# Normalising x by token, evacuating the projection on ScalarE, and turning plain x inside the mix product

## The chip, the core and the metric

One NeuronCore of a Trainium2 chip runs the whole program. Its engines are TensorE (PE, with its weight loads PEld), VectorE (DVE), ScalarE (ACT), GpSimd (POOL) and SyncE (SP, which only issues DMAs here; ACT issues some too). The metric is the device time of one execution in microseconds, as a median over runs: 3062.14 us for the kernel before (three runs, 3060.99 to 3066.02).

## What is computed

One encoder block, float32, on 2048 tokens of width 1024, with 256 memory tokens:

```python
h = rmsnorm(x, mix_norm_w);  proj = h @ w_in          # 1024 -> 3072: q k v g a b, 512 each
y_ret  = retention_group(q, k, v, g, ...)             # 4 heads of 128, both directions, chunks of 128
y_conv = conformer_conv_group(a, b, ...)              # a*sigmoid(b), 31-tap depthwise conv, layernorm, silu
x = x + concat([y_ret, y_conv]) @ w_out               # "mix"
x = x + cross_attention(rmsnorm(x), rmsnorm(mem))     # 4 heads of 256, 256 memory tokens
x = x + square(relu(rmsnorm(x) @ w_ff1)) @ w_ff2      # 1024 -> 4096 -> 1024
return rmsnorm(x, final_norm_w)
```

Each big product keeps float32 accuracy by splitting both sides in a high and a low part: hi*hi, hi*lo and lo*hi, so 24 matmuls of 128x128 by 512 columns for one 128x512 output ("a GEMM" below).

## The kernel before

Activations lie with features on partitions and tokens along the free axis: 8 tiles of features (k), 4 chunks of 512 tokens (n). Five instruction streams are written by hand; every order is explicit and is kept by semaphores. Weights come as 128x1024 blocks through two slots `wraw`; POOL splits each block (`split_weights`, L505: `whi` L511, `wlo` L513), and a slot's turn comes when the block before it in that slot has been used.

**Prologue** (L283 to L350, L673 to L696, L1013 to L1035, L1366 to L1386). x is loaded in token-major halves of chunks (`xt`), turned by PE (L679), and each turned tile in PSUM is read four times: ACT makes `xhi` (times the norm weight, L1022) and squares it (`sq0`, L1024), DVE copies plain x to `xf` (L1371, which SP stores to `xT_d`, L350) and makes `xlo` (L1372); POOL adds the squares (L543). The same is done for mem. PE sums the squares over features (L692), ACT and DVE turn that into 1/rms as a full tile `rs` (L1033, L1383). The first projection GEMM comes after all of it (L696). x in these products is not normalised.

**Projection** (L701 to L768, a loop over 4 heads c). `ORDER` (L55) lists the items of a head: six groups of four GEMMs (a, b, q, k, v, g), memory products V and K (256 columns), O (values through `w_xo`) T and M (`w_xq` turned and multiplied by the keys). PSUM banks 0 to 3 are used in turn, one semaphore `bank_free` in order; banks 4 to 7 hold O and M. DVE evacuates every GEMM with `ps * rs` (`evac`, L1393), into `upad` for a, into `st` for the others; ACT then stores `st` to `proj_d` (L1042), or takes the sigmoid of b (L1087), and DVE multiplies a by it (L1464). Between these DVE runs the 31 taps of the convolution (`tap`, L1419), two after each evacuation. DVE also makes the low parts of K and V (`low`, L1403), of w_xq (`query_low`, L1407) and of the stored products (`made_low`, L1415). `values_out` (L713) waits for `w_ready`, that is the low part too; `keys_in` (L740) waits for `query_low`.

**Retention and convolution** (L772 to L866). The loads of k, its swapped halves, v, q, q swapped and g for head 0 are issued by SP from L393 on, after the last store of the memory products (L390). sin and cos are loaded earlier (L386).

**Two halves of 1024 tokens** (L876 to L990): mix (`product`/`mix`, L881 to L899), `scores`, attention, out product, MLP. Mix adds into `res`, which ACT fills beforehand with plain x from `xT_d` (`load_residual`, L1231; L1316 for the second half). SP loads the keys of attention head 0 as soon as the weights of mix are through (L462). At the start of the MLP, PE waits for the sum of squares and runs `stats` (L966) ahead of the first GEMM.

Of the kernel before, what the change touches and what calls it, by code (L numbers as in the profile page):

```python
# [20 lines left out]
def build(nc, x, mem, positions, mix_norm_w, w_in, ret_decay_f, ret_decay_b, ret_gn_w, ret_gn_b,  # L21
# [30 lines left out]
    G_MEM = NS * KT  # L52
    G_PROJ = G_MEM + KT
# [8 lines left out]
    SLOT = {"a": 0, "V0": 1, "b": 1, "V1": 0, "q": 0, "K0": 1, "k": 1, "K1": 0, "O0": 0, "v": 0, "O1": 1, "Q0": 1, "g": 1, "Q1": 0}  # L62
# [4 lines left out]
    G_HALF0 = G_PROJ + HEADS * GP  # L67
# [13 lines left out]
    xT_d = nc.dram_tensor("xT_d", [KT, P, NS, NC], F32).ap()  # L81
# [9 lines left out]
    with es:  # L91
# [31 lines left out]
        with ExitStack() as s1:  # L123
            xhi = alloc(s1, "xhi", [P, KT, NS, NC], F32R)
            xlo = alloc(s1, "xlo", [P, KT, NS, NC], F32R)
            rs = alloc(s1, "rs", [P, NS, NC], F32)
            rsm = alloc(s1, "rsm", [P, M], F32)
            kz = alloc(s1, "kz", [P, M], F32)
            mhi = alloc(s1, "mhi", [P, KT, M], F32R)
            mlo = alloc(s1, "mlo", [P, KT, M], F32R)  # L130
            with ExitStack() as s0:
                xt = alloc(s0, "xt", [P, 2, 4, D // 2], F32)
                memt = alloc(s0, "memt", [P, 2, D], F32)
                alloc(s0, "gap", [P, 32], F32)
                xf = alloc(s0, "xf", [P, 4, NC], F32)
                sq0 = alloc(s0, "sq0", [P, 2, NC], F32)
                vrow, trow = xf[:, 0, 0:P], xf[:, 1, 0:P]
# [8 lines left out]
            upad = alloc(s1, "upad", [P, S + 2 * PAD + 2], F32)  # L146
            acc = alloc(s1, "acc", [P, S], F32)
# [31 lines left out]
        with ExitStack() as s3:  # L179
# [8 lines left out]
            res = b3("res", (P, KT, NH, NC))  # L188
            wb = b3("wb", (P, 2, KT, P), F32R)
# [19 lines left out]
        x_in = [sem("x_in0"), sem("x_in1")]  # L209
        mem_in = sem("mem_in")  # L210
        hi0, sq0_done, ssq_done = sem("hi0"), sem("sq0_done"), sem("ssq_done")
        xf_done = sem("xf_done")
        xf_st = [sem(f"xf_st{n}") for n in range(4)]
        stat_mm, stat_sq, stat_rc = sem("stat_mm"), sem("stat_sq"), sem("stat_rc")
        sig_done, u_done, pad_ok = sem("sig_done"), sem("u_done"), sem("pad_ok")
        conv_step, acc_st = sem("conv_step"), sem("acc_st")
        st_st = [sem(f"st_st{n}") for n in range(NS)]
        kv_hi, kv_lo = sem("kv_hi"), sem("kv_lo")
# [6 lines left out]
        def released(eng, g):  # L225

            eng.wait_ge(bank_free, g + 1 + G0)

# [40 lines left out]
        r_in = [sem(f"r_in{k}") for k in range(KT)]  # L269
# [14 lines left out]
        def _(sp):  # L284
            start_at_one(sp, *xf_st)

# [5 lines left out]
            xr = x.rearrange("b (n s p) d -> n p (b s) d", s=4, p=P)  # L292
            for s in range(2):
                sp.dma_start(xt[:, s, :, :], xr[0, :, :, s * (D // 2):(s + 1) * (D // 2)]).then_inc(x_in[s], 16)
            sp.wait_ge(x_in[0], 16)
            sp.dma_start(memt[:, :, :], mem.rearrange("b (s p) d -> p (b s) d", p=P)).then_inc(mem_in, 16)
            sp.dma_start(freq[:, :], rope_freq).then_inc(tab_in, 16)
            sp.dma_start(dec[:, 0, :], ret_decay_f[0:1, :].to_broadcast([P, HEADS])).then_inc(dec_in, 16)
            sp.dma_start(dec[:, 1, :], ret_decay_b[0:1, :].to_broadcast([P, HEADS])).then_inc(dec_in, 16)
# [7 lines left out]
            def split_of(c, name):  # L307
                sp.wait_ge(w_ready, BP * c + SPLIT[name] + 3)
# [4 lines left out]
            def first_two(c):  # L313
                columns(0, in_cols(c, "a"))
                if not isinstance(c, int):
                    split_of(c - 1, "g")
                columns(1, w_xkv[0, :, bass.ds((KT + 2 * c) * P, P)])

            def proj_loads(c):
                split_of(c, "V0")  # L320
                columns(1, in_cols(c, "b"))
                split_of(c, "a")
# [3 lines left out]
                split_of(c, "b")  # L326
                columns(1, w_xkv[0, :, bass.ds(2 * c * P, P)])
                split_of(c, "K0")
                columns(1, in_cols(c, "k"))
                split_of(c, "q")  # L330
                columns(0, w_xkv[0, :, bass.ds((2 * c + 1) * P, P)])
                split_of(c, "K1")
                rows_of(0, w_xo[0, bass.ds(2 * c * P, P), :])
                split_of(c, "O0")
                columns(0, in_cols(c, "v"))
                split_of(c, "k")
                rows_of(1, w_xo[0, bass.ds((2 * c + 1) * P, P), :])
                split_of(c, "O1")
                columns(1, w_xq[0, :, bass.ds(2 * c * P, P)])
                sp.wait_ge(mm_done, G_PROJ + GP * c + GI["T0"] + 2)  # L340
                columns(1, in_cols(c, "g"))
                split_of(c, "v")
                columns(0, w_xq[0, :, bass.ds((2 * c + 1) * P, P)])

            first_two(0)

            with sp.Fori(0, NS) as n:
                for k in range(KT):
                    sp.wait_ge(xf_done, KT * n + k + 1)
                    sp.dma_start(xT_d[k, :, n, :], xf[:, k % 4, :]).then_inc(xf_st[k % 4], 16)  # L350
            proj_loads(0)
            with sp.Fori(1, HEADS) as c:
                sp.wait_ge(mm_done, G_PROJ + GP * (c - 1) + GI["T1"] + 2)
                first_two(c)
                proj_loads(c)
            for s in range(4):
                sp.wait_ge(xf_st[s], 1 + 16 * NS * KT // 4)
# [30 lines left out]
            sp.wait_ge(m_mm, 1 + 2 * HEADS)  # L388
            for s in range(2):
                sp.wait_ge(pre_st[s], 1 + 16 * 4 * HEADS)  # L390
            for n in range(NS):
                sp.wait_ge(st_st[n], 1 + 16 * 4)
            load_k(0)  # L393
# [6 lines left out]
            sp.wait_ge(acc_st, 1 + 16 * HEADS)  # L400
# [43 lines left out]
            for h in range(2):  # L444
                J = J_HALF0 + J_PER_HALF * h
                with sp.Fori(1 - h, KT // 2) as i:
                    for s in range(2):
                        load_weights(J + 2 * i + s, s, w_out[0, :, bass.ds((2 * i + s) * P, P)])
# [14 lines left out]
                sp.wait_ge(phase, 5 * 2)  # L463
# [27 lines left out]
        def _(pool):  # L491
# [12 lines left out]
            pool.wait_ge(vec_ok, 2)  # L504
# [15 lines left out]
            def done(c, item):  # L520
                return G_PROJ + GP * c + GI[item] + 1

            proj_split(0, "a", None)
            proj_split(0, "V0", None)

            def proj_splits(c):
                proj_split(c, "b", done(c, "V0"))
                proj_split(c, "V1", done(c, "a3"))
                proj_split(c, "q", done(c, "V1"))
                proj_split(c, "K0", done(c, "b3"))  # L530
                proj_split(c, "k", done(c, "K0"))
                proj_split(c, "K1", done(c, "q3"))
                proj_split(c, "O0", done(c, "K1"))
                proj_split(c, "v", 1 + 2 * c + 1, o_mm)
                proj_split(c, "O1", done(c, "k3"))
                proj_split(c, "g", 1 + 2 * c + 1, m_mm)

            for n in range(NS):
                for k in range(KT):
                    g = KT * n + k  # L540
                    pool.wait_ge(sq0_done, g + 1)
                    pool.wait_ge(ssq_done, g + 2)
                    pool.tensor_tensor(rs[:, n, :], rs[:, n, :], sq0[:, k % 2, :], ALU.add).then_inc(ssq_done, 1)  # L543
            proj_splits(0)
            with pool.Fori(1, HEADS) as c:
                proj_split(c, "a", 1 + 2 * c, m_mm)
# [98 lines left out]
        def _(pe):  # L645
# [27 lines left out]
            with pe.Fori(0, NS) as n:  # L673
                for k in range(KT):
                    if k % 4 == 0:
                        pe.wait_ge(x_in[k // 4], 16 * n + 16)
                    bank_ready(KT * n + k)
                    for t in range(4):
                        last = pe.transpose(ps[:, k % 4, t * P:(t + 1) * P],  # L679
                                            xt[:, k // 4, t, (k % 4) * P:(k % 4 + 1) * P], ident[:, :])  # L680
                    last.then_inc(mm_done, 1)
            pe.wait_ge(mem_in, 16)
            for k in range(KT):
                bank_ready(G_MEM + k)
                for t in range(2):
                    last = pe.transpose(ps[:, k % 4, t * P:(t + 1) * P], memt[:, t, k * P:(k + 1) * P], ident[:, :])
                last.then_inc(mm_done, 1)

            pe.wait_ge(vec_ok, 2)
            for n in range(NS):  # L690
                pe.wait_ge(ssq_done, 2 + KT * (n + 1))
                pe.matmul(ps[:, 4 + n, :], mean_mat[:, :], rs[:, n, :], start=True, stop=True).then_inc(stat_mm, 1)  # L692
# [1096 lines left out]
```

## Time and profile before

| | us |
|---|---|
| median of the runs | 3062.14 |
| the profiled execution | 3065.82 |
| its span, first to last instruction | 3064.0 |
| PE busy / DVE / ACT / POOL | 2844.2 / 1514.4 / 517.3 / 954.9 |

The page gives, for each engine, the busy time and its share of the span, then the chain of work that ended last. The traces show by stage (times from the start of the span): prologue to 83, projection to 737, retention and convolution to 1025, first half to 2047 and second half to the end, each beginning with mix.

### The profile page before, as it was taken

What the parts mean: (1) busy time and instruction counts of PE and PEld (TensorE: products, weight loads), DVE (VectorE), ACT (ScalarE), POOL (GpSimd) and SP (SyncE); (2) the same over time, 40 slices, a digit from 0 to 9 for tenths busy, and PEclk for the clock granted to TensorE, in tenths of its full rate; (3) what the DMA queues carried; (4) which work ended last, traced back from release to release, by engine and by line L of the source; (5) the groups of instructions that cost most, each with busy time, mean ns of one, the idle gap of its engine ahead of it and who ended that gap; (6) DMA issues with size and microseconds to landing.
All of it is one profiled execution on the core that took longest, in us unless ns stands there. A gap on an engine that the chain in (4) does not pass through costs nothing.

```text
span 3064.0 us, 37737 instructions
## 1 busy us (share of the span) xinstructions
PE 2844.2 (93%) x13772; PEld 2365.7 (77%) x13772; DVE 1514.4 (49%) x1688; ACT 517.3 (17%) x890; POOL 954.9 (31%) x500
## 2 busy tenths in 40 slices
PE   4999999996777799999999999989999999999997
PEld 3878787875655589878888888868987888888886
DVE  6685858686675543352332414455335324142344
ACT  5201010101444322210000101122221000010012
POOL 6242424241664300033333333321002333333331
PEclk6999999998889899999999999999999999999998
DMA  7133332326633322211111111341221111111111
GB/s 249 58 109 118 103 110 95 134 72 203 202 127 131 110 90 83 76 41 48 48 48 48 48 48 48 103 144 69 83 84 47 48 48 48 48 48 48 48 48 62
DMA packets 281925, 262.04 MB, mean 86 GB/s; under 512 B 8400, under 2 KB 237960, under 8 KB 275592
## 3 DMA queue, kind: packets, MB, share of 16 engines
q1 hardware_dynamic: 252464, 192.96, 20.5%
q10 hardware_dynamic: 29400, 68.26, 6.1%
q8 instruction: 38, 0.62, 0.1%
q14 instruction: 23, 0.19, 0.0%
HBM read 196.71 MB, written 64.49 MB: 85 GB/s over the span
## 4 chain that ended last, share of the span: by engine, by line
PE 81%; DVE 7%; POOL 4%; issue 3%; DMA 2%; ACT 2%; DVEq 0%; ACTq 0%; SPq 0%; POOLq 0%
PE ps L660 24%; PE ps L655 23%; PE ps L656 23%; PE ps L917 2%; PE ps L919 2%; PE ps L918 2%; POOL wlo L513 1%; DVE acc L1429 1%; POOL whi L511 1%; DMA xt<-in_x 1%; DMA q_sw<-proj_d 1%; DVE alo L1584 1%; DMA out<-rows 1%; POOL cv L585 1%; DVE st_b L1547 1%
## 5 line engine op out<-in xcount | busy, mean ns | idle before, releaser
L511 POOL TENSOR_SCALAR whi<-wraw 128x1024 fp32r<-128x1024 f32 x192 | 233.1, 1214 | 1877.8 <-PE ps L660 1222.6
L655 PE MATMUL ps<-ahi,whi 128*128 128x512 f32 x1408 | 553.1, 393 | 33.2 <-DVE alo L1584 20.7
L656 PE MATMUL ps<-alo,whi 128*128 128x512 f32 x1408 | 549.8, 391 | 0.0
L513 POOL TENSOR_TENSOR wlo<-wraw,whi 128x1024 fp32r<-128x1024 f32 x192 | 528.6, 2753 | 16.0
L655 PE MATMUL ps<-bhi,whi 128*128 128x512 f32 x1024 | 401.1, 392 | 0.0
L656 PE MATMUL ps<-blo,whi 128*128 128x512 f32 x1024 | 399.2, 390 | 0.0
L660 PE MATMUL ps<-ahi,wlo 128*128 128x512 f32 x1408 | 349.6, 391 | 0.0
L1729 DVE TENSOR_TENSOR res<-ps,res 128x512 f32 x128 | 88.6, 692 | 519.6 <-PE ps L660 519.6
L655 PEld LDWEIGHTS ps<-ahi,whi 128*128 128x128 f32 x1408 | 265.4, 189 | 98.7 <-DVE alo L1584 20.4
L1429 DVE SCALAR_TENSOR_TENSOR acc<-upad,taps,acc 128x2048 f32<-128x2048 f32 x120 | 323.9, 2700 | 6.4 <-DVE acc L1426 0.6
L660 PEld LDWEIGHTS ps<-ahi,wlo 128*128 128x128 f32 x1408 | 265.4, 189 | 55.6
L656 PEld LDWEIGHTS ps<-alo,whi 128*128 128x128 f32 x1408 | 265.7, 189 | 54.3 <-issue 0.2
L655 PE MATMUL ps<-xhi,whi 128*128 128x512 f32 x768 | 300.2, 391 | 0.0
L656 PE MATMUL ps<-xlo,whi 128*128 128x512 f32 x768 | 299.2, 390 | 0.0
L1295 ACT ACTIVATE ahi<-z 128x512 f32 x128 | 80.9, 632 | 1153.5 <-DVE z L1714 1153.5
L660 PE MATMUL ps<-bhi,wlo 128*128 128x512 f32 x1024 | 252.9, 389 | 0.0
L655 PEld LDWEIGHTS ps<-bhi,whi 128*128 128x128 f32 x1024 | 193.1, 189 | 41.2 <-issue 1.0
L656 PEld LDWEIGHTS ps<-blo,whi 128*128 128x128 f32 x1024 | 192.9, 188 | 41.0 <-issue 1.0
L1717 DVE TENSOR_TENSOR alo<-z,ahi 128x512 f32 x128 | 164.8, 1287 | 119.1 <-ACT ahi L1295 119.1
L660 PEld LDWEIGHTS ps<-bhi,wlo 128*128 128x128 f32 x1024 | 192.2, 188 | 39.9
L1712 DVE TENSOR_TENSOR z<-ps,rstd 128x512 f32<-128x512 f32 x128 | 88.6, 692 | 229.4 <-PE ps L660 228.2
L660 PE MATMUL ps<-xhi,wlo 128*128 128x512 f32 x768 | 189.7, 389 | 0.0
(253 smaller groups left out, 3772.0 us busy)
## 6 DMA issues: line engine op xcount, KB each, us to landing
wraw<-in_w_ff SPq DMA_DIRECT2D x128, 512.0 KB, 3.9
proj_d<-st ACTq DMA_DIRECT2D x64, 256.0 KB, 2.4
wraw<-in_w_in SPq DMA_DIRECT2D x24, 512.0 KB, 4.1
wraw<-in_w_xkv SPq DMA_DIRECT2D x16, 512.0 KB, 5.2
xT_d<-xf SPq DMA_DIRECT2D x32, 256.0 KB, 4.7
vwo_d<-pst ACTq DMA_DIRECT2D x16, 512.0 KB, 3.4
wqk_d<-pst ACTq DMA_DIRECT2D x16, 512.0 KB, 3.4
wraw<-in_w_out SPq DMA_DIRECT2D x16, 512.0 KB, 3.9
```

The costliest lines, as they stand in the source:

```text
L511: pool.tensor_scalar(whi[:, slot, :, :], wraw[:, slot, :, :], 1.0, 0.0, ALU.mult, ALU.add).then_inc(w_hi, 1)
L513: pool.tensor_tensor(wlo[:, slot, :, :], wraw[:, slot, :, :], whi[:, slot, :, :], ALU.subtract).then_inc(w_ready, 1)
L655: nc.tensor.matmul(o, whi[:, slot, k, :], hi(k), start=(k == order[0]), stop=False)
L656: nc.tensor.matmul(o, whi[:, slot, k, :], lo(k), start=False, stop=False)
L660: last = nc.tensor.matmul(o, wlo[:, slot, k, :], hi(k), start=False, stop=(k == order[-1]))
L917: pe.matmul(o, a, high[:, k * M:(k + 1) * M], start=(k == 0), stop=False)
L918: pe.matmul(o, a, low[:, k * M:(k + 1) * M], start=False, stop=False)
L1295: act.activation(ahi[:, 2 * i + s, n, :], z[:, n, :], ACT.Copy).then_inc(hi_done, 1)
L1429: ins = dve.scalar_tensor_tensor(out=acc[:, :], in0=src, scalar=taps[:, bass.ds(CT * t + c, 1)], in1=acc[:, :], op0=ALU.mult, op1=ALU.add)
L1712: dve.tensor_tensor(z[:, n, :], ps[:, 2 * s + n, :], rstd[:, n, :], ALU.mult).then_inc(bank_free, 1)
L1717: dve.tensor_tensor(alo[:, 2 * i + s, n, :], z[:, n, :], ahi[:, 2 * i + s, n, :], ALU.subtract).then_inc(lo_done, 1)
L1729: dve.tensor_tensor(res[:, m, n, :], ps[:, 2 * s + n, :], res[:, m, n, :], ALU.add).then_inc(bank_free, 1)
```

## The change

**Prologue.** x is loaded as whole rows (512 KB a transfer), four of them a chunk, into two chunk buffers. While tokens lie on partitions, ACT squares each row with an accumulated sum (`square`), takes the root, DVE the reciprocal, and DVE and POOL scale two tiles of 128 tokens each (`scale_x`). Only then PE turns it (into banks 4 to 7), ACT makes `xhi`, DVE `xlo`. `rs`, `rsm`, `kz`, `xf`, `sq0`, `xT_d` and the statistics go. The projection of head 0 starts when chunk 0 is ready; the other turns stand in PE's queue between its first GEMMs. The decay constants (Exp, Ln) move behind the prologue on ACT and DVE.

**Projection.** The order is b before a, and K, O, T, M are moved. ACT evacuates b (directly through Sigmoid) and q, k, v, g (Copy); DVE takes a times the gate, and the low parts straight from PSUM. Each bank has its own semaphore. All taps run in a row with the low parts between them. `values_out` does its hi products with `w_hi` alone.

**Hand-over.** sin, k and k swapped are loaded after the last M, cos right behind; v, q, g as before.

**Mix.** SP loads plain x, token-major, one 128-feature column block of a half (`xs`, 512 KB); PE turns it into banks 4 to 7 (four transposes for each GEMM), ACT copies it to `res`. `xs` lies over `wb`, so the keys of attention head 0 are loaded after the last turn.

**MLP.** `stats` comes behind the first GEMM.

The core of the diff:

```diff
-    ORDER = ["a0", "a1", "V0", "a2", "a3", "b0", "b1", "V1", "b2", "b3", "q0", "q1", "K0", "q2", "q3",
-             "k0", "K1", "k1", "k2", "O0", "k3", "v0", "O1", "v1", "T0", "v2", "M0", "v3",
-             "g0", "T1", "g1", "M1", "g2", "g3"]
+    ORDER = ["b0", "b1", "V0", "b2", "b3", "a0", "a1", "V1", "a2", "a3", "q0", "q1", "O0", "q2", "q3",
+             "k0", "k1", "O1", "k2", "k3", "v0", "v1", "K0", "T0", "v2", "M0", "v3",
+             "g0", "g1", "K1", "T1", "g2", "M1", "g3"]
...
             sp.wait_ge(tab_st, 1 + 32 * HEADS)
-            sp.wait_ge(kv_lo, 1 + 4 * HEADS)
+            sp.wait_ge(m_mm, 1 + 2 * HEADS)
+            sp.wait_ge(acc_st, 1 + 16 * HEADS)
...
             sp.dma_start(sin_t[:, :], tab_d[0]).then_inc(l_tab, 16)
+            load_k(0)
+            sp.wait_ge(mm_done, GP * (HEADS - 1) + GI["K1"] + 1)
             sp.dma_start(cos_t[:, :], tab_d[1]).then_inc(l_tab, 16)
...
+                sp.wait_ge(phase, 5 * 2)
+                for i in range(KT // 2):
+                    for s in range(2):
+                        m = 2 * i + s
+                        if h or i:
+                            load_weights(J + m, s, w_out[0, :, m * P:(m + 1) * P])
+                    for s in range(2):
+                        m = 2 * i + s
+                        if h or i:
+                            sp.wait_ge(xr_mm, 16 * h + 4 * i + 2 * s - 2)
+                        sp.dma_start(xs[:, s, :, :], x[0, h * HALF:(h + 1) * HALF, m * P:(m + 1) * P].rearrange("(t p) d -> p t d", p=P)
+                                     ).then_inc(xs_in[s], 16)
...
+                sp.wait_ge(xr_mm, 16 * h + 16)
                 load_keys(0)
...
+                    if isinstance(c, int):
+                        if item == "b0":
+                            turn_x(0, 0, 2)
+                            pe.wait_ge(xt_free, KT)
+                        elif item == "b1":
+                            turn_mem()
+                            turn_x(1, 2 * KT, 5)
+                            pe.wait_ge(xt_free, 3 * KT)
+                        elif kind == "b":
+                            turn_x(n, KT * (n + 1), 2 * n + 3)
+                            pe.wait_ge(xt_free, KT * (n + 2))
...
+                def turn_residual(i, s, n, h):
+
+                    if n == 0:
+                        pe.wait_ge(xs_in[s], 64 * h + 16 * i + 16)
+                    for t in range(4):
+                        tr = pe.transpose(ps[:, 4 + 2 * s + n, t * P:(t + 1) * P], xs[:, s, 4 * n + t, :], ident[:, :])
+                    tr.then_inc(xr_mm, 1)
...
                 if h == 0:
-                    mix(0, ready=split_done)
-                with pe.Fori(1, KT // 2) as i:
+                    mix(0, ready=split_done, turns="behind")
+                else:
+                    mix(1, turns="behind")
+                with pe.Fori(1 + h, KT // 2) as i:
                     mix(i)
...
+                up(0, 0, mlp_sums)
...
+            def square(src, to, done):
+                if done >= 2:
+                    act.wait_ge(x_sq, done - 1)
+                act.activation(sqj[:, done % 2, :], src, ACT.Square, accum_out=ssx[:, to:to + 1]).then_inc(x_sq, 1)
...
-                high("V0", vhl[:, 0, 0, :])
...
+                gate(0)
+                gate(1)
+                wait_alone(act, o_mm, 1 + 2 * c)
                 high("V0", vhl[:, 0, 0, :])
+                gate(2)
+                gate(3)
...
+                        act.activation(st[:, n, :], src, ACT.Copy).then_inc(left, 1)
...
+                            wait_alone(act, xr_mm, 16 * half + e + 1)
+                            act.activation(res[:, 2 * i + s, n, :], ps[:, 4 + idx, :], ACT.Copy).then_inc(xr_cp, 1)
...
+                taps_of(0, 16)
+                made_low(0)
+                made_low(1)
+                taps_of(16, 18)
+                made_low(2)
+                made_low(3)
+                taps_of(18, 24)
+                low("K0", 2, khl[:, 0])
+                query_low(0)
+                taps_of(24, TAPS)
+                low("K1", 3, khl[:, 1])
+                query_low(1)
+                for m in range(4, 8):
+                    made_low(m)
```

## Rows read from the trace of the kernel before

**Rows 1.** The page, part 1: busy us, share of the span, instructions.

```profile
PE 2844.2 (93%) x13772; PEld 2365.7 (77%) x13772; DVE 1514.4 (49%) x1688; ACT 517.3 (17%) x890; POOL 954.9 (31%) x500
```

**Rows 2.** Stretches: length; PE, PEld, DVE, ACT, POOL busy (count); clock, DMA share, GB/s.

```profile
25.00:50.00 25.00, 14.81 (x56) 10.42 (x56) 19.53 (x30) 19.13 (x33) 22.26 (x18) 0.50 0.90 291
...
393.00:557.00 164.00, 158.59 (x762) 133.33 (x761) 119.91 (x89) 15.61 (x25) 60.78 (x24) 0.98 0.32 107
...
750.00:780.00 30.00, 12.30 (x94) 12.10 (x95) 14.89 (x25) 15.77 (x33) 12.97 (x8) 0.70 1.02 281
...
1310.00:2012.00 702.00, 696.22 (x3067) 575.18 (x3066) 254.11 (x273) 50.22 (x80) 227.13 (x126) 1.00 0.18 53
```

**Rows 3.** PE's waits from 83.3 to 735: us in total, times, longest.

```profile
PE ps L725 <- POOL wlo L513: 14.1, 4, 3.5
PE ps L752 <- DVE wlo L1412: 4.1, 4, 1.0
PE ps L752 <- DVE pst L1417: 3.5, 4, 0.9
```

**Rows 4.** PE in order of time, prologue: start, us, instruction, idle before it.

```profile
12.41 0.33 PE L669 MATMUL ps<-ident,xf 60*128 60x60 f32 x1 [12.41 <-DMA xf<-in_conv_w]
...
45.46 4.48 PE L679 MATMUL ps<-ident,xt 128*128 128x128 f32 x16 [1.52 <-DMA xt<-in_x]
...
83.36 0.58 PE L655 MATMUL ps<-xhi,whi 128*128 128x512 f32 x1
...
108.26 0.39 PE L655 MATMUL ps<-xhi,whi 128*128 128x512 f32 x1
```

**Rows 5.** ACT and DVE by line and form: busy us, mean ns, idle before.

```profile
L1229 ACT ACTIVATE ahi<-y_stage 128x1024 fp32r<-128x1024 f32 x16 | 15.4, 1041 | 0.0
L1271 ACT ACTIVATION_READ_ACCUMULATOR sq<-ps,nb,rtx 128x1 f32 x64 | 12.4, 194 | 0.0
L1010 ACT ACT_TABLE_LOAD x1 | 1.3, 1283 | 0.0
L1372 DVE SCALAR_TENSOR_TENSOR xlo<-ps,vec,xhi 128x512 f32 x32 | 23.8, 744 | 0.0
L1426 DVE TENSOR_SCALAR acc<-upad,taps,vec 128x2048 f32<-128x2048 f32 x4 | 5.4, 1340 | 0.0
```

**Rows 6.** The tap's line: duration in ns, min/median/max.

```profile
L1429 DVE SCALAR_TENSOR_TENSOR acc<-upad,taps,acc x120: 2335/2352/4264, 141.4 to 739.4; 128x2048 f32<-128x2048 f32 x120
```

**Rows 7.** POOL in order of time: one low part of a weight block, beside DVE's taps.

```profile
345.34 4.31 POOL L513 TENSOR_TENSOR wlo<-wraw,whi 128x1024 fp32r<-128x1024 f32 x1
```

**Rows 8.** Hand-over to retention, in order of time.

```profile
743.64 0.33 SPq L363 DMA_DIRECT2D k_in<-proj_d  x1
...
757.55 4.49 POOL L554 TENSOR_TENSOR k_sw<-k_sw,sin_t 128x2048 f32<-128x2048 f32 x1 [45.20 <-DMA k_sw<-proj_d]
...
769.73 5.07 POOL L603 TENSOR_TENSOR q_sw<-q_sw,sin_t 128x2048 f32<-128x2048 f32 x1 [6.94 <-DMA q_sw<-proj_d]
```

**Rows 9.** Start of mix, in order of time.

```profile
1025.38 0.79 PE L655 MATMUL ps<-ahi,whi 128*128 128x512 f32 x1 [11.44 <-DVE alo L1584]
...
1026.40 3.62 PE L660 MATMUL ps<-ahi,wlo 128*128 128x512 f32 x8
...
1030.66 0.06 DVE L1623 MEMSET junk<- 128x1 f32 x1 [5.33 <-SPq L237]
```

**Rows 10.** DMA issues: KB each, us from issue to landing (page; then 1092 to 1108).

```profile
wraw<-in_w_out SPq DMA_DIRECT2D x16, 512.0 KB, 3.9
...
wb<-wqk_d SPq DMA_DIRECT2D x1, 1024.0 KB, 6.8
```

**Rows 11.** Eight transposes at the full clock, in order of time.

```profile
716.10 1.03 PE L737 MATMUL ps<-ident,wraw 128*128 128x128 f32 x8
```

**Rows 12.** Statistics ahead of the MLP, in order of time.

```profile
1305.80 3.78 PE L874 MATMUL ps<-ssq,mean_mat 128*128 128x512 f32 x4 [4.86 <-DVE ssq L1640]
```

**Rows 13.** Between the halves, in order of time.

```profile
2062.62 0.69 DVE L1634 TENSOR_TENSOR res<-ps,res 128x512 f32<-128x512 f32 x1 [14.63 <-PE ps L987]
```

More of the change, by code:

```diff
@@ L188, in build @@
             res = b3("res", (P, KT, NH, NC))
+            with ExitStack() as over:
+                xs = b3("xs", (P, 2, 8, P), F32, over)
             wb = b3("wb", (P, 2, KT, P), F32R)
@@ L678, in _ @@
                     for t in range(4):
[L679 to L692, printed above, removed]
-            pe.wait_ge(ssq_done, 2 + KT * (NS + 1))
-            pe.wait_ge(stat_sq, 1)
-            pe.matmul(ps[:, 4, 0:M], mean_mat[:, :], rsm[:, :], start=True, stop=True).then_inc(stat_mm, 1)
-            released(pe, G_PROJ - 1)
+                        tr = pe.transpose(ps[:, 4 + k % 4, t * P:(t + 1) * P], xt[:, n % 2, t, k * P:(k + 1) * P], ident[:, :])
@@ L698, in flat, with turn_mem, projections, bank_taken @@
+                    tr.then_inc(xt_mm, 1)
+            def turn_mem():
+                pe.wait_ge(x_low, 3)
+                pe.wait_ge(x_high, 3)
+                for k in range(KT):
+                    pe.wait_ge(xt_free, KT + k - 3)
+                    for t in range(2):
+                        tr = pe.transpose(ps[:, 4 + k % 4, t * P:(t + 1) * P], memt[:, t, k * P:(k + 1) * P], ident[:, :])
+                    tr.then_inc(xt_mm, 1)
             def flat(w, slot):
                 return w[:, slot, :, :].rearrange("p k m -> p (k m)")
-            with pe.Fori(0, HEADS) as c:
+            def projections(c):
+                def bank_taken(g):
+                    if not isinstance(c, int) or g >= 4:
+                        pe.wait_ge(proj_free[g % 4], PB * c + g // 4)
@@ L879, in _, with product @@
                 H = H_PER_HALF * h
-                def product(i, g, j, hi, lo, ready, order=range(KT)):
+                def product(i, g, j, hi, lo, ready, order=range(KT), behind=None, ahead=None):
                     for s in range(2):
@@ L885, in product, with mix, turn @@
                             bank_ready(g + 4 * i + 2 * s + n)
+                            if ahead is not None:
+                                ahead(s, n)
                             gemm(2 * s + n, s, lambda k: hi[:, k, n, :], lambda k: lo[:, k, n, :], NC,
                                  ready if s == 0 and n == 0 else None, order, j + 2 * i + s if n == 0 else None)
[L890 to L891 removed]
+                            if behind is not None:
+                                behind(s, n)
+                def turn_residual(i, s, n, h):
+                    if n == 0:
+                        pe.wait_ge(xs_in[s], 64 * h + 16 * i + 16)
+                    for t in range(4):
+                        tr = pe.transpose(ps[:, 4 + 2 * s + n, t * P:(t + 1) * P], xs[:, s, 4 * n + t, :], ident[:, :])
+                    tr.then_inc(xr_mm, 1)
+                def mix(i, h=h, ready=None, turns="ahead"):
+                    def turn(s, n):
+                        turn_residual(i, s, n, h)
+                    product(i, G_HALF0 + G_PER_HALF * h, J_HALF0 + J_PER_HALF * h, ahi, alo, ready, Y_ORDER,
+                            turn if turns == "behind" else None, turn if turns == "ahead" else None)
                 def split_done(k, h=h):
@@ new lines, in _, with taps_of @@
+                gated(0)
+                gated(1)
+                low("V1", 1, vhl[:, 1])
+                gated(2)
+                gated(3)
+                bank_left(dve, c, "a3")
+                def taps_of(first, last):
+                    for t in range(first, last):
+                        tap(t)
+                taps_of(0, 16)
[5 more added lines that the diff above has]
+                taps_of(18, 24)
@@ L1628, in _, with residual @@
                 Q = Q_PER_HALF * h
-                def residual(i, g, hb, qb, norm, order=S_FIRST):
+                def residual(i, g, hb, qb, norm, order=S_FIRST, half=None):
                     for idx, (s, n) in enumerate(order):
```

520 lines of the change are left out of this document (248 added, 272 removed).

## The prediction

> **What bounds the kernel now.** I read the page's busy shares first: PE is busy 93% of the span [rows 1]. The table of stretches then says where the other 7% lies. In the MLP PE issues 3067 matmuls in 702 us at clock 1.00, 0.229 us each, so a GEMM of 24 is 5.5 us [rows 2]; nothing is to be gained there, and what the change adds to PE in such places is paid in full. The idle time is in five other places, and a sum of the change is a walk through them.
>
> Prologue: the first projection GEMM starts at 83.36, and until then PE turns tiles at half clock (0.50 from 25 to 50), waiting for the engines that read them [rows 2, 4]. Head: the four heads wait 14.1 + 4.1 + 3.5 = 21.7 us in all, 5.4 each, on POOL's low part of the O block and on DVE [rows 3]; 158.59 busy of 164 in one head says the same [rows 2]. Hand-over to retention, start of mix, statistics before the MLP, end of a half: rows 8, 9, 12 and 13.
>
> **Prologue: -14 us (bounds -20 and -9).** Removed: copies of plain x, squares from PSUM, POOL's sums, the statistics. PE has the norm vectors at 12.4 [rows 4], about when ACT may begin. Four squares of 128x1024 at 1.04 + 0.19 for the accumulator read are 4.9; root with its table load 1.5; the reciprocal 0.2; DVE scales two tiles at half of 1.34 each, POOL its two by about 2.1 [rows 5], the small ones by the nearest form. PE turns chunk 0 from 22 on, 16 transposes taking no less than 4.48 less their waits [rows 4], so 32 take 7, plus one pass of ACT and DVE (0.7 + 0.74) [rows 5]: b0 starts near 31. Its first microseconds are at half clock: 38.5. Then mem (3.6) and chunk 1 (0.65 to 0.86 for each of 8 tiles, plus 1.7) come before b1, chunk 2 before b2, chunk 3 before b3. POOL's split of a stands behind four scalings in its queue, and is not needed before a0. One wait is new: b3 takes bank 0, which ACT frees only with its first Sigmoid, and in front of that on ACT stand Exp, Ln and Sigmoid with a table load of 1.28 each [rows 5], DVE's nine small steps and the load of positions: about 6 us after the last tile. I get b3 finished, and a0 started, at 88 if PE stays at the full clock between the GEMMs and at 99.6 if it falls each time (each GEMM + 2.5, each chunk 8.6 instead of 6.9). Before, four such GEMMs and a memory product were done at 108.26 [rows 4]. The gain is thus 20 or 9; I take 14.
>
> On ACT's table loads the trace and the Trainium skill differ. ScalarE: Activation LUTs, What ACT_TABLE_LOAD costs, has a drain of 1.38 us with each, which would add about 4 us here; the row of the trace shows 1283 ns and nothing idle ahead of it [rows 5], and the measurement decides.
>
> **Heads: -13 us (bounds -20 and 0).** Sixteen Copies of 0.6 us a head move to ACT, which is busy 15.61 of 164 [rows 2]; they are covered. Of the waits, the 3.5 on O's low part goes: O follows two GEMMs after its slot is free, and a split lasts 6.7 beside the taps (4.31 for its low part [rows 7]). What is late next is DVE at M0. In a head's own time M0 is due after 19 GEMMs, three memory products, both O and T0: 119.4. DVE starts the taps at 50.3 after a3 and has in front of `query_low(0)`: one tap of 1.34 [rows 5], 23 of 2.35 [rows 6], four `made_low` of 0.69, and five splits of POOL in that time. Beside a split the two engines lengthen each other: the tap goes from 2.35 to 4.26 [rows 6], so 1.9 a split. 50.3 + 1.3 + 54.1 + 2.8 + 9.5 + 1.7 = 119.7, and with gaps between taps PE waits about 1.9 a head: 7.6 for the four, where 21.7 were lost; 13 after rounding down. ACT is blocked in its queue from O1 (88) until DVE reaches `made_low(1)` (97), with the evacuations of k2 and k3 behind it, but their banks are wanted only at 110 and 113. No stall at all is the upper bound (-20), a wait as long as now the lower.
>
> **Hand-over: -9 us (bounds -11 and 0).** The load of k is issued at 743.64, 6.4 after PE ends (737.3); k swapped is used at 757.55, q swapped at 769.73 [rows 8]: 32.4 after the end. After: sin, k, k swapped and cos are issued 5.4 before the end. They are 4 MB, with 1 MB of stores among them. Then the last stores land at +11, and v, q and q swapped are issued. At the rate of the second stretch (281 GB/s with all queues full [rows 2]) their 3 MB take 12: q swapped at +23. But sin and cos, 2 MB, were loaded long before and now lie in the crowded time; if everything is bound by bytes, 2 MB at that rate give back 7.5, and with the stores all of it: 0.
>
> **Start of mix: +7 us (bounds 0 and +8).** Covered so far: nothing waits for plain x. After, PE must turn the first `xs` tile behind the first GEMM. That GEMM ends at 1026.40 + 3.4 = 1029.8; SP passes the phase at 1030.66 [rows 9], and a 512 KB block of such rows lands 3.9 after its issue [rows 10]: 1034.7. So 4.9 idle, and as the clock has been at half until then (3.62 for 8 matmuls, 0.45 each [rows 9]), about 2.2 more before it rises.
>
> **Turns in mix: +13.9 us (bounds +11 and +24).** 128 transposes, 16 of them counted under the end of the half. Eight take 1.0 at the full clock [rows 11], 0.124 each: 112 x 0.124. At half clock they would take twice that. ACT's copy (0.6) is covered, it has 1.4 us of other work for each 5.5.
>
> **Keys: +3.8 us (bounds 0 and +7).** The load of head 0's keys now waits for the last turn, one GEMM before mix ends. Its second megabyte lands 6.8 after its issue [rows 10], plus 0.5 for the first issue: 5.5 of 7.4 are covered, 1.9 are not, twice.
>
> **End of half 0: +1.3 us (bounds -3 and +5).** PE's last transposes end at 2062.6 and DVE's add starts there [rows 13]. After, ACT must have copied the last rows, PE turns 16 tiles (2.0) and ACT and DVE pass one; against this the residual's 4 MB no longer delay the output stores.
>
> **Statistics: -11.6 us (bounds -15 and -7).** PE waits 4.86 for the last sum and then runs four matmuls in 3.78 at half clock [rows 12]. Behind the first GEMM the sum is ready and the clock is up: 4.86 + 1.9, and 1.4 for the cold start of the GEMM, less 2.4 for the weights and low parts for which that GEMM now waits itself: 5.8 a half. The later 1/rms is not missed: DVE frees the first bank at +17, PE wants it at +24.
>
> **Sum.** -14 - 13 - 9 + 7 + 13.9 + 3.8 + 1.3 - 11.6 = -21.6. The profiled execution took 3065.82 (its span is 3064.0), 3.7 over the median; the sum gives 3044.2 against it, and 3040.5 against the median.
>
> **The rivals.** (a) Everything opens: warm prologue (-20), no stall in the heads (-20), hand-over -11. That is 15 more: 3025.5. For it: each is a bound that rows allow. (b) The clock stays down through the whole alternation of turns and GEMMs in the prologue (-9): 3045.5. For it: from 25 to 50 PE is busy 14.81 of 25 and is granted 0.50 all along, also through 16 transposes in a row [rows 2, 4]. By the Trainium skill (TensorE: Matmul & The Clock Gate, Part 4: PE-mode transpose) a transpose does not count as busy for the clock; by that rule this is the case, and the trace agrees so far. Against it: each stretch of turns is only 7 to 11 us long. (c) The hand-over is bound by bytes and gives nothing, with the cold prologue: 3040.5 + 9 + 5 = 3054.5. For it: DMA share 1.02 there [rows 2]. (d) Slower: DVE is late at M0. Were DVE to stand still for half of each split (3.35 of 6.7) instead of losing 1.9, that is 1.45 more for each of five, 7.3 a head, 29 in all: 3069.5. The change loses by over 0.2% from the point where DVE arrives some 9 us after M0 is due, and gains nothing from 7 on. Against it: the median tap is 2352 ns, and only the extreme 4264 [rows 6]. (e) The prologue's b3 waits far longer for its bank, or a new order stalls in a way no row shows.
>
> **Chances.** Forecast 0.50 (3030 to 3050), (a) 0.14, (b) 0.12, (c) 0.11, (d) 0.09, (e) 0.04. The range reaches from somewhat below (a) to just past (c), and leaves out (d) and (e): 3018 to 3062. About 0.2% (6 us) is what a measurement of this kernel can tell from no change: faster by more than that is the forecast, (a), (b) and part of (c), 0.80; within it the rest of (c) and a part of (d) and (e), 0.12; slower the rest of those, 0.08.
>
> **What would show it.** Prologue: the fifth group's first GEMM (a0) between 88 and 100, b3 preceded by a wait for ACT's Sigmoid. Heads: no wait at `values_out`, one of 1 to 3 us at M0 on DVE. Hand-over: POOL on q swapped 23 to 25 after PE's end. Mix: a wait of 5 on a DMA behind the first GEMM, 0.5 more for each GEMM. Attention: a wait of about 2 on the keys. MLP: no wait of 4.86. What would make it wrong: a wait at M0 of 7 or more, or GEMMs at half clock beyond the first 100 us.

## The result

The changed kernel takes 3074.1 us (median of eight runs, 3071.1 to 3075.1), the kernel before 3064.1 (eight runs, 3061.0 to 3068.5): ratio 1.0031, 95% interval 1.0020 to 1.0042. It is slower by 0.3%, some 9.5 us. The forecast was 3040.5 in a range of 3018 to 3062, made from the first three of the eight runs before (3062.1): the sign is wrong, and the time lies outside the range. The profiled execution of the changed kernel took 3074.24, its span is 3072.2.

The page of the changed kernel, part 1 (busy us, share, instructions), against [rows 1]:

```profile
PE 2841.1 (92%) x13890; PEld 2372.5 (77%) x13890; DVE 1431.3 (47%) x1543; ACT 566.5 (18%) x979; POOL 940.0 (31%) x477
```

PE has 118 instructions more and is busy 3 us less, DVE 83 less: the work moved as intended. So the time went into waits. PE in order of time in the changed kernel (start, us, instruction, idle before it), one row for each border of a stage:

```profile
102.15 0.39 PE L670 MATMUL ps<-xhi,whi 128*128 128x512 f32 x1
...
727.74 1.98 PE L675 MATMUL ps<-xhi,wlo 128*128 128x512 f32 x8
...
1018.53 0.79 PE L670 MATMUL ps<-ahi,whi 128*128 128x512 f32 x1 [11.63 <-DVE alo L1649]
...
1028.49 1.12 PE L931 MATMUL ps<-ident,xs 128*128 128x128 f32 x4 [5.32 <-DMA xs<-in_x]
...
1037.27 0.48 PE L670 MATMUL ps<-ahi,whi 128*128 128x512 f32 x1
...
1122.33 0.39 PE L969 MATMUL ps<-wrr,bhi 128*128 128x256 f32 x1 [1.77 <-DMA wb<-wqk_d]
...
1319.54 0.80 PE L670 MATMUL ps<-bhi,whi 128*128 128x512 f32 x1
...
2068.57 0.50 PE L670 MATMUL ps<-ahi,whi 128*128 128x512 f32 x1 [0.40 <-DVE res L1701]
...
2339.72 0.80 PE L670 MATMUL ps<-bhi,whi 128*128 128x512 f32 x1
```

The same borders in the kernel before: 108.26 [rows 4], 1025.38 [rows 9], and these:

```profile
735.68 1.97 PE L660 MATMUL ps<-xhi,wlo 128*128 128x512 f32 x8
...
1035.70 0.39 PE L655 MATMUL ps<-ahi,whi 128*128 128x512 f32 x1
...
1111.86 0.28 PE L917 MATMUL ps<-wrr,bhi 128*128 128x256 f32 x1
...
1315.44 0.39 PE L655 MATMUL ps<-bhi,whi 128*128 128x512 f32 x1
...
2063.45 0.49 PE L655 MATMUL ps<-ahi,whi 128*128 128x512 f32 x1 [0.87 <-DVE res L1634]
...
2332.01 0.39 PE L655 MATMUL ps<-bhi,whi 128*128 128x512 f32 x1
```

The difference of two neighbouring borders, against the term of the sum:

| stage | before, ends at | after, ends at | change | predicted |
|---|---|---|---|---|
| prologue, to the fifth projection GEMM | 108.26 | 102.15 | -6.1 | -14 |
| heads, to the last GEMM's last part | 735.68 | 727.74 | -1.8 | -13 |
| hand-over and retention, to mix | 1025.38 | 1018.53 | +1.1 | -9 |
| start of mix, to its third GEMM | 1035.70 | 1037.27 | +8.4 | +7, and 1 for eight turns |
| rest of mix, keys, half 0 | 1111.86 | 1122.33 | +8.9 | +7 and +1.9 |
| scores to the MLP's second GEMM | 1315.44 | 1319.54 | -6.4 | -5.8 |
| MLP and end of half 0 | 2063.45 | 2068.57 | +1.0 | +1.3 |
| mix to second MLP GEMM, half 1 | 2332.01 | 2339.72 | +2.6 | +2.1 |

From mix on the prediction gave +14.4, and the trace shows +15.0 to the end of the span. Ahead of mix it gave -36, and the trace shows -6.9. Nearly all of the error, 29 of 29.8 us, lies in three stages. PE's waits in the changed kernel up to 735 name what is late in two of them (us in total, times, longest):

```profile
PE ps L770 <- DVE wlo L1501: 21.7, 4, 5.4
PE ps L684 <- DMA trow<-in_conv_w: 16.1, 1, 16.1
PE ps L698 <- POOL xt L536: 14.2, 2, 12.9
PE ps L670 <- ACT st L1139: 7.5, 1, 7.5
```

The wait on O's low part [rows 3] is gone, as predicted. In its place PE waits for DVE at M0 (L770), 5.4 a head: by coincidence the very 21.7 that were lost before.

### The profile page after: what moved, and what is told of

The parts are those of the page before. It is cut to its first block, busy times and chain, and to the rows that moved or that the text cites. A ratio compares the mean times of both kernels' runs of the same rounds, so it can differ in the third digit from the quotient of the medians.

```text
span 3072.2 us, 37360 instructions
## 1 busy us (share of the span) xinstructions
PE 2841.1 (92%) x13890; PEld 2372.5 (77%) x13890; DVE 1431.3 (47%) x1543; ACT 566.5 (18%) x979; POOL 940.0 (31%) x477
## 4 chain that ended last, share of the span: by engine, by line
PE 75%; DVE 14%; issue 3%; DMA 2%; ACT 2%; POOL 2%; DVEq 0%; ACTq 0%; SPq 0%; POOLq 0%
PE ps L675 22%; PE ps L670 22%; PE ps L671 21%; DVE acc L1516 7%; PE ps L969 2%; PE ps L971 2%; PE ps L970 2%; DVE zfin L1808 1%; POOL cv L600 1%; DVE alo L1649 1%; PE ps L873 1%; DMA wqk_d<-pst 1%; DVE st_b L1612 1%; DVE alo L1782 0%; PE ps L980 0%
## 5 line engine op out<-in xcount | busy, mean ns | idle before, releaser
L1516 DVE SCALAR_TENSOR_TENSOR acc<-upad,taps,acc 128x2048 f32<-128x2048 f32 x120 | 346.7, 2889 | 15.7 <-DVE acc L1513 0.6
```

Source lines behind the costliest of these rows:

```text
L1516: ins = dve.scalar_tensor_tensor(out=acc[:, :], in0=src, scalar=taps[:, bass.ds(CT * t + c, 1)], in1=acc[:, :], op0=ALU.mult, op1=ALU.add)
```

## The experiments

Ratios are to the kernel before, run beside each; the changed kernel has 1.0031. A difference of two ratios is turned into us with 3064.

**Heads, where the low parts stand.** The low part of K0 and `query_low(0)` after tap 20 instead of tap 24:

```diff
-                taps_of(18, 24)
+                taps_of(18, 20)
                 low("K0", 2, khl[:, 0])
                 query_low(0)
-                taps_of(24, TAPS)
+                taps_of(20, TAPS)
```

> The changed kernel, with the low part of K0 and query_low(0) four taps earlier in DVE's order (after tap 20 instead of 24); nothing is left out. In the changed kernel PE waits 5.4 us at M0 in each head for that low part, 21.7 in all. Theory (DVE is late at M0 only because of where its taps stand): it arrives 4 x 2.35 = 9.4 us sooner and no sooner than ACT's half of the turned w_xq (354.87 in the second head), so the wait at M0 goes wholly, and as DVE then reaches query_low(1) at 389.0 where M1 is due near 391, nothing takes its place: 21.7 less, 3052.4 us, and M0 shows no wait on DVE above 0.5. Rival (the 31 taps with their splits bound the stretch from a3 to M1 as a whole): the wait moves to M1, 3 to 5 us a head, and the time stays within 5 us of 3074.

Measured: 3047.7, ratio 0.9947 (0.9934 to 0.9961), 26 us less than the changed kernel: more than the 21.7 of waiting. PE at M0 in the second head of the changed kernel, and in this one:

```profile
365.10 0.58 PE L770 MATMUL ps<-khl,whi 128*128 128x256 f32 x1 [5.42 <-DVE wlo L1501]
...
369.37 0.40 PE L670 MATMUL ps<-xhi,whi 128*128 128x512 f32 x1
```

```profile
351.55 0.28 PE L770 MATMUL ps<-khl,whi 128*128 128x256 f32 x1
...
354.42 0.40 PE L670 MATMUL ps<-xhi,whi 128*128 128x512 f32 x1
```

After the stall M0's 24 matmuls take 4.3 us here and 5.3, 5.0 and 5.3 in the other three heads, without it 2.9: a wait of 5.4 costs 6.8 to 7.8, since the granted clock behind it is 0.50 (365 to 368). That gives 30 in place of 21.7; 5.2 come back as a wait of 1.3 a head at M1, and 1.1 of the gain lies ahead of the edit (a0 starts at 101.07 instead of 102.15). The rival is out.

**What a split costs DVE.** POOL does both steps of block k's split twice:

```diff
+                if twice is not None:
+                    pool.tensor_scalar(whi[:, slot, :, :], wraw[:, slot, :, :], 1.0, 0.0, ALU.mult, ALU.add).then_inc(again, 1)
+                    wait_alone(pool, again, twice)
                 pool.tensor_scalar(whi[:, slot, :, :], wraw[:, slot, :, :], 1.0, 0.0, ALU.mult, ALU.add).then_inc(w_hi, 1)
```

and the same for the second step.

> The changed kernel, with POOL doing both steps of one split a head (that of block k, which lies beside the taps with 8 us to spare before its first GEMM) twice; the second pass writes the same values. It measures what one split costs DVE's tap run, and so the wait at M0 (5.4 now). Theory from the trace of the changed kernel: 23 taps took 68.0 us where 23 x 2.35 is 54.1, for five splits, 2.8 each, since a tap is lengthened beside the first step of a split as well as beside the second. Then the wait at M0 goes to 8.2, each head is 2.8 longer, and the time 11 us: 3085. Rival (the term of the prediction: one tap of 4.26 instead of 2.35 for a split, 1.9): wait 7.3, 7.6 us in all: 3081.7. Second rival (POOL's passes cost DVE nothing, the taps are long for another reason): no change, 3074.

Measured: 3079.0, ratio 1.0047 (1.0032 to 1.0063), 4.9 more; the waits at M0 are 27.0 in all, 1.3 more a head. The interval in time (up to 9.8 more) holds the second number too, but the wait grew by less than either theory said, and not by nothing. DVE's taps one by one show what a split does to them (start, us, from the chain of this kernel):

```profile
306.67 2.91 DVE acc L1523
309.71 2.92 DVE acc L1523
312.76 4.27 DVE acc L1523
317.17 4.27 DVE acc L1523
```

The changed kernel has one of each there:

```profile
302.49 2.36 DVE acc L1516
304.99 2.92 DVE acc L1516
308.04 4.27 DVE acc L1516
312.44 2.36 DVE acc L1516
```

So a split lengthens two taps: the one beside its first step by 0.56, the one beside its second by 1.91, 2.47 together, and the doubled split costs that once more. From the first tap to `query_low(0)` DVE takes 74.44 us instead of 72.16, 2.28 more in each head; so the price of a split lies between the two theories. The wait grew by only 1.3 because PE itself came to M0 0.9 later after the first tap. Of that, 0.6 is a new wait a head, for a bank that ACT evacuates late:

```profile
356.57 0.50 PE L677 MATMUL ps<-xhi,whi 128*128 128x512 f32 x1 [0.58 <-ACT st L1139]
...
369.06 0.58 PE L777 MATMUL ps<-khl,whi 128*128 128x256 f32 x1 [6.76 <-DVE wlo L1508]
```

The term of 1.9 had seen the second step of a split only. POOL pays as well, in order of time in the changed kernel: 1.04 becomes up to 2.94, and 2.39 becomes 4.31, 1.9 longer each.

```profile
315.28 2.94 POOL L521 TENSOR_SCALAR whi<-wraw 128x1024 fp32r<-128x1024 f32 x1 [5.12 <-PE ps L675]
318.29 4.31 POOL L523 TENSOR_TENSOR wlo<-wraw,whi 128x1024 fp32r<-128x1024 f32 x1
```

This is what the Trainium skill says in SBUF — State Buffer, Who interferes with whom: a DVE instruction with two SBUF inputs and a GpSimd instruction that reads SBUF take the same port by turns, and the second to start stands still until the first has ended. The rows agree: the two engines' instructions alternate, each waiting for the other's. Read so, the first step of a split had to have a price of its own.

**Prologue, who scales.** All rows of x and mem are scaled by DVE, none by POOL:

```diff
-            scale_x(0, 1)
             proj_split(0, "b", None)
...
                 dve.wait_ge(x_rc, which)
-                for t in range(2):
+                for t in range(4):
```

> The changed kernel, with all scalings of x and mem by their 1/rms on DVE and none on POOL; nothing is left out. In the changed kernel POOL's two of a chunk take 6.2 to 6.6 us beside 2.3 for DVE's two, and PE starts to turn when POOL is done (29.69, 47.53, 65.14, 81.81). Theory (POOL's 3.1 us for a tile scaled by a column is what holds the prologue): with four at 0.7 on DVE the turns of the chunks start at about 25.6, 42, 58.5 and 71, and a0 at 91.6 instead of 102.2: 10.6 us less, 3063.5. Rival (the squares on ACT and the landing of x hold it just as long): only chunk 0 gains, 4 us: 3070. Second rival (b3's wait for its bank, 7.5 now, takes up what the last chunk gains): about 7 us, 3067.

Measured: 3062.8, ratio 0.9999 (0.9990 to 1.0008), 9.8 less by the ratios. POOL and PE in the changed kernel, then DVE and PE in this one:

```profile
22.90 6.64 POOL L536 TENSOR_SCALAR xt<-xt,rx 128x1024 f32<-128x1024 f32 x2 [20.01 <-DVE rx L1440]
29.69 5.87 PE L698 MATMUL ps<-ident,xt 128*128 128x128 f32 x32 [12.88 <-POOL xt L536]
...
81.81 5.68 PE L698 MATMUL ps<-ident,xt 128*128 128x128 f32 x32 [4.09 <-issue]
...
95.00 0.76 PE L670 MATMUL ps<-xhi,whi 128*128 128x512 f32 x1 [7.52 <-ACT st L1139]
```

```profile
22.89 2.74 DVE L1430 TENSOR_SCALAR xt<-xt,rx 128x1024 f32<-128x1024 f32 x4
25.78 5.68 PE L686 MATMUL ps<-ident,xt 128*128 128x128 f32 x32 [8.90 <-DVE xt L1430]
...
85.22 0.77 PE L659 MATMUL ps<-xhi,whi 128*128 128x512 f32 x1 [7.51 <-ACT st L1126]
```

POOL's two tiles take 6.6, DVE's four 2.7. Most of it is POOL's own: its last tile of the fourth chunk, started when DVE was done, still took 2.84, against 3.3 to 3.4 beside DVE; PE's wait of 4.09 ends with it. The first theory holds; a0 starts 9.0 sooner.

**Hand-over, a wait behind the loads.**

```diff
-            for s in range(2):
-                sp.wait_ge(pre_st[s], 1 + 16 * 4 * HEADS)
             sp.wait_ge(mm_done, G_HALF0)
             load_v(0)
             load_q(0)
             load_g(0)
+            for s in range(2):
+                sp.wait_ge(pre_st[s], 1 + 16 * 4 * HEADS)
```

> The changed kernel, with SP's wait for the last stores of w_xq times keys put behind the issue of the loads of v, q and g instead of ahead of it; nothing is left out. In the changed kernel these loads are issued at 745.65 and after, 16 us after PE's last GEMM (729.5), and POOL starts on q swapped at 760.87, 31.4 after that GEMM; the stores lie in the queues with the 4 MB of sin, k, k swapped and cos. Theory (the wait in SP's order holds the loads): they are issued at 730, 15 us sooner, and the 9 MB from 724.3 on at some 330 GB/s are through at about 752: q swapped at 752 to 754, 7 to 9 us less, 3066. Rival (bytes bind the stretch, or the stores land later by what the loads gain and hold the phase): gain of 0 to 2, 3073.

Measured: 3066.0, ratio 1.0007 (0.9998 to 1.0016), 7.4 less. SP and POOL in the changed kernel, then in this one:

```profile
745.65 0.33 SPq L369 DMA_DIRECT2D v_in<-proj_d  x1
...
760.87 4.52 POOL L618 TENSOR_TENSOR q_sw<-q_sw,sin_t 128x2048 f32<-128x2048 f32 x1 [15.16 <-DMA q_sw<-proj_d]
```

```profile
730.55 0.33 SPq L369 DMA_DIRECT2D v_in<-proj_d  x1
...
752.15 4.56 POOL L618 TENSOR_TENSOR q_sw<-q_sw,sin_t 128x2048 f32<-128x2048 f32 x1 [5.62 <-DMA q_sw<-proj_d]
```

PE's last GEMM ends at 729.5 and 730.4: q swapped is there 31.4 after it with the wait, 21.8 without.

**Statistics, undone.** `stats` ahead of the first GEMM of the MLP again:

```diff
+                stats(h, Q_PER_HALF * h + 32, lambda: pe.wait_ge(p_exp, 32 * h + 32 + 4))
+
                 def up(i, g, behind=None):
...
-                up(0, 0, mlp_sums)
+                up(0, 0)
```

> The changed kernel, with the statistics of the MLP ahead of its first GEMM again, as in the kernel before; nothing is left out. From the end of mix to the second GEMM of the MLP the kernel before takes 1315.44 - 1111.86 = 203.6 us and the changed one 1319.54 - 1122.33 = 197.2. Theory (this step of the prediction, 5.8 a half, was right, and what the half loses it loses elsewhere): 6.4 come back in each half: 12.8 more, 3086.9, with a wait of 4.9 on the sum of squares in each half. Rival (the gain comes from the scores, where the load of the keys moved, and not from the statistics): less than 4 us more, 3076.

Measured: 3083.9, ratio 1.0072 (1.0055 to 1.0089), 12.6 more. The wait is back:

```profile
1313.05 3.78 PE L907 MATMUL ps<-ssq,mean_mat 128*128 128x512 f32 x4 [4.87 <-DVE ssq L1705]
```

**Start of mix.** The first turns of plain x behind the second GEMM:

```diff
                     def turn(s, n):
+                        if turns == "behind" and h == 0:
+                            if s == 0 and n == 0:
+                                return
+                            if s == 0:
+                                turn_residual(i, 0, 0, h)
                         turn_residual(i, s, n, h)
```

> The changed kernel, with the first four transposes of plain x in the first half behind the second GEMM of mix instead of the first; nothing is left out. In the changed kernel PE waits 5.3 us behind its first GEMM for the load of that x, and then runs at half clock until 1033.7, where the kernel before is at the full clock 5.3 us after its first matmul of mix. Theory (the load lands at 1028.4, when the second GEMM would end): 5.3 of waiting and 1.6 to 2 us of half clock go: 6.9 to 7.3 less, 3067. Rival (the clock does not rise sooner): 5.3 less, 3068.8. Second rival (the wait moves to the second turns, whose x lands later, or to DVE's add): less than 3 us, 3072.

Measured: 3067.9, ratio 1.0009 (1.0000 to 1.0019), 6.7 less. PE:

```profile
1019.10 0.79 PE L670 MATMUL ps<-ahi,whi 128*128 128x512 f32 x1 [11.47 <-DVE alo L1654]
...
1029.44 1.03 PE L931 MATMUL ps<-ident,xs 128*128 128x128 f32 x8
1030.23 0.48 PE L670 MATMUL ps<-ahi,whi 128*128 128x512 f32 x1
```

From mix's first matmul to its third GEMM 11.1 us instead of 18.7; the wait and the half clock are gone.

**More of the prologue.** On top of the scalings on DVE: ACT's wait for the vectors behind its squares, and Exp and Ln of the decay constants ahead of its last high parts:

```diff
-            act.wait_ge(vec_ok, 1)
-
             def square(src, to, done):
...
             root(16, 18, 6)
+            act.wait_ge(vec_ok, 1)
...
+                if n == NS - 1:
+                    act.wait_ge(dec_dve, 1)
+                    act.activation(lg[:, 1], lg[:, 0], ACT.Exp, scale=-1.0).then_inc(dec_act, 1)
```

> The kernel with all scalings on DVE (3062.8), with two more edits in the prologue: ACT no longer waits for the norm vectors before it squares the first rows of x, and the Exp and Ln of the decay constants stand ahead of ACT's last eight high parts of x instead of behind them; nothing is left out. In that kernel ACT sits idle until 16.77 for the vectors, and DVE is free of them at 17.2; b3 waits 7.5 us for the bank that ACT leaves with its first Sigmoid, behind two table loads of 1.28. Theory (both are on the path to a0): DVE scales from 17.3 instead of 22.9, PE turns from 20.2 instead of 25.8, 5.6 less; and ACT reaches the Sigmoid 3.0 after its last high part instead of 6, 3 less: a0 at 84.7 instead of 93.3, 3054.2. Rival (x or the weights of b land too late, or the next chunks' loads do): only the second edit counts, 3 us, 3060.

Measured: 3057.3, ratio 0.9981 (0.9972 to 0.9991), 5.5 less than with the scalings alone; a0 starts 6.4 sooner, of 8.6 expected. PE turns from 19.93 on, as expected, but then (the last row is a stretch: length; PE, PEld, DVE, ACT, POOL busy; clock, DMA share, GB/s):

```profile
19.89 4.11 DVE L1443 TENSOR_SCALAR memt<-memt,rx 128x1024 f32<-128x1024 f32 x2
...
24.71 3.26 PE L686 MATMUL ps<-ident,xt 128*128 128x128 f32 x16 [1.51 <-DVE xlo L1435]
29.54 0.79 PE L659 MATMUL ps<-xhi,whi 128*128 128x512 f32 x1 [1.56 <-DVE xlo L1435]
...
78.52 0.76 PE L659 MATMUL ps<-xhi,whi 128*128 128x512 f32 x1 [3.06 <-ACT st L1126]
...
24.00:29.00 5.00, 3.26 (x16) 2.38 (x16) 4.90 (x8) 3.05 (x6) 0.00 (x0) 0.71 0.02 4
```

DVE's two tiles of mem, 1.4 before, take 4.1, with POOL's split of V0 now beside them, and hold up the low parts; and b0 takes 7.15 (29.54 to 36.69) instead of 5.6, partly at half clock: the granted clock falls while PE still turns chunk 0, to a mean of 0.71 from 24 to 29, and is 0.50 from 29 to 31. Why it falls there, and not in the changed kernel, was not settled.

**Together.** The edits of the first, third and fourth kernel of this section (heads, prologue, hand-over), and the low part of K1 and `query_low(1)` two taps earlier:

> The three edits that gained alone, together (low part of K0 and query_low(0) after tap 20; scalings of x on DVE; the wait for the last stores behind the loads of v, q and g), and the low part of K1 and query_low(1) two taps earlier as well, for the 1.3 us that PE still waits at M1 in each head of the first of them; nothing is left out. Theory (prologue, heads and hand-over are three separate places, each with its own late step): the gains add: 3074.1 - 26.4 - 11.3 - 8.1 = 3028, and 4 x 1.3 less at M1, less up to 2 that come back because the last head's taps are stored later and sin is loaded over them: 3024. Rival (one place shows what another hid, for example the shorter heads make the loads of the hand-over meet the stores of the last head): 8 us or more above the sum, 3036.

Measured: 3031.0, ratio 0.9894 (0.9875 to 0.9914), 7 over the theory and 5 under the rival, whose 0.991 lies in the interval while the theory's 0.987 lies just outside. In the stretch from 266 to 429, about a head (length; PE, PEld, DVE, ACT, POOL busy; clock, DMA share, GB/s), the changed kernel and this one:

```profile
266.00:429.00 163.00, 157.58 (x765) 133.55 (x764) 106.96 (x60) 24.87 (x42) 59.59 (x25) 0.99 0.32 108
```

```profile
266.00:429.00 163.00, 163.00 (x796) 138.07 (x795) 107.47 (x61) 24.09 (x40) 59.74 (x25) 1.00 0.32 108
```

PE has no idle time left in a head. But in the hand-over sin is issued 3.1 before PE's end (686.88, 690.0) instead of 5.2, because the last taps are stored later, and q swapped is used 25.7 after it, not 21.8. That is the rival's mechanism, yet little of these 4 us reaches mix: from the last GEMM's last part to mix it takes 285.2 (688.19 to 973.38), against 284.1 in the kernel of the hand-over alone (728.55 to 1012.62), and the theory had allowed 2 for it. Of the 7 us over the theory 2.9 are the theory's own: it took the differences of medians (26.4, 11.3, 8.1), where the ratios give 25.7, 9.8 and 7.4. The other 4 are not accounted for; they lie within the interval (3025.7 to 3037.6).

**All of them**, with DVE's scaling of mem behind its low parts of chunk 0:

> All edits that gained, in one kernel: those of the three together (3031.0), the first turns of mix behind its second GEMM (6.7 less than the changed kernel, by their ratios to the kernel before), the two of the prologue (5.5 less than with the scalings alone), and DVE's scaling of mem behind its low parts of chunk 0, since beside POOL's split its second tile took 3.4 us instead of 0.7 and held those low parts up; nothing is left out. Theory (five places, each with its own late step): 3031.0 - 6.7 - 5.5 - 1.5 = 3017.3, that is 1.5% under the kernel before. Rival (what comes earlier is waited for at the next place): 6 us or more above that sum, 3023 to 3028.

Measured: 3012.4 (3008.7 to 3015.1), ratio 0.9827 (0.9813 to 0.9840): 5 us below the theory's sum and 1.7% under the kernel before, with every part of the change kept.

## Why the prediction was wrong

**Prologue (-14; -6.1).** The mechanism was right, two sizes and one landing were wrong. "POOL its two by about 2.1" took the price of POOL's `whi` step, whose operands are constants, for a scaling by a column: a form that [rows 5] lacks; it measures 6.6, and it stood before each chunk, 4.5 us at the first and 1.3, 1.4 and 4.1 of PE's waiting at the others. "PE has the norm vectors at 12.4" [rows 4]: after, with 6 MB of loads issued in the first 8 us, it is 16.1. So b0 started at 37.5, not 31. b3's wait for its bank is 7.5, not 6. The bound of 99.6 failed though it held the half clock for every stretch, and that came only in part: b0 ran in 5.6 us, and the stretch from 29 to 37, with nothing but 32 transposes on PE, had a granted clock of 1.00, where the kernel before had 0.50 from 25 to 50 [rows 2]. The clock was at 0.50 from 48 to 50, from 82 to 84 and from 92 to 98, so that b3 took 7.15 (95.00 to 102.15), and at 1.00 from 51 to 81. Rival (b), half clock all through, is out.

```profile
29.00:37.00 8.00, 5.80 (x32) 5.35 (x32) 5.16 (x8) 5.69 (x9) 6.75 (x4) 1.00 0.08 7
```

By the rule of the Trainium skill that the prediction quoted (TensorE: Matmul & The Clock Gate, Part 4: PE-mode transpose) b0 would have begun at half clock; here it did not. The rows don't decide on the rule: the granted clock was 1.00 already from 16 to 29, when PE ran two matmuls, so it was not the turns that raised it. In the kernel of "More of the prologue" the turns start 9.8 us sooner, the clock falls while they run, and b0 does begin at half clock, as it would by that rule.

**Heads (-13; -1.8).** The step that failed is DVE's arrival at `query_low(0)`, 119.7 against a due time of 119.4. What is late next was named rightly, M0, and the due time was right within 1 us: PE was there 68.1 us after DVE's first tap, where 69.1 was put. DVE was there 73.5 us after it (291.60 to 365.05 in the second head), not 69.4. The five splits lengthened the 23 taps in front of M0 by 11.2 us (65.3 busy instead of 54.1), where 9.5 was put, and the gaps between DVE's instructions took 2.6, where 1.6 were allowed. DVE is thus 2.4 later than the 71.0 with its gaps, and PE 1.0 sooner: a wait of 5.4 instead of 1.9. This is rival (d) at half its size. It had a chance of 0.09 because its price was argued against from the median tap; the extreme one [rows 6] was one of two a split, not an exception. Each stall also costs 1.4 to 2.4 of half clock, which no term had. The kernel before pays that too: its granted clock is 0.58 from 194 to 197, behind its wait of 3.5. A head lasts 163.6 in it, 162.9 in the changed kernel and 155.2 in the kernel of three edits, where no wait is left. So 5.4 us of waiting a head were worth 8.4 and 7.7, and with no stall the four heads would have gained some 33, not the 20 of the upper bound.

**Hand-over (-9; +1.1).** "Then the last stores land at +11" failed: they landed at +16, and SP's own wait for them held v and q. The two stores issued at 725.85, among 4 MB of loads, took up to 14.7 us to land, where the same stores took 2.8 to 4.5 in the kernel before; and the last two products could be made only when the buffers of these came free, so that their stores were issued from 741.30 on. That there are two rounds of stores, the second behind the landing of the first, the term did not have. The experiment shows the rest of the step to be right (+21.8 against +23).

**Start of mix, turns, keys, end of the half, statistics (+14.4; +15.0).** All held: 5.32 for 4.9 of waiting, 0.50 for each four transposes (a GEMM lasts 5.94 instead of 5.44), 1.77 and 1.91 on the keys for 1.9, +1.0 for +1.3, -6.4 for -5.8. These are the stages that were priced from rows of the same operations in the trace of before.

**The range** was centred on a sum in which three late steps each had a margin of a few us, and a missed price in each went the same way. With the three measured stages put in, the sum is -6.1 - 1.8 + 1.1 + 14.4 = +7.6; the span grew by 8.2.

## What to carry to other kernels

Price a moved elementwise step by its own form on its own engine, operand kind included; where no row has it, the bound is wide. Where two engines take turns at one port, every instruction of the other engine that reads SBUF can have a price for the first, not only the longest. After a change that packs a stream densely, compute the slack of each consumer inside it, and put the consumer's part before the last point where it is due: here that was two lines, and worth 26 us.

## What the runs showed that was not expected

A scaling of 128x1024 by a column takes 2.84 to 3.41 us on POOL (eight of them) and 0.68 on DVE; the same shape with constants takes POOL 1.04. A stall of 5.4 us on PE costs 1.4 to 2.4 more in half clock behind it (M0 in the four heads). And DVE's scaling, though it has one tensor input, is also held by POOL's split: 4.1 for two tiles beside it (in the kernel of "More of the prologue"), 1.4 without (with the scalings alone).
